# RWKV time mixing: input splits ahead of the keys, banks per first chunk, decays by group, the finish in pieces, and the gate's linears beside the last levels and the last state chain

## The chip, the cores and the metric

The kernel runs on one core of a Trainium2 chip. The metric is the device time of one execution in microseconds (us), as the median of several runs. Everything is computed in 32 bits; where this text says "split", a float32 operand is held as a rounded high part and the remainder (low part), and a product takes three matmuls (high x high, low x high, high x low).

## What is computed

One token sequence of 272 tokens (16 meta tokens and 256 inputs) and 1024 features goes through two blocks of feed-forward, mixer, feed-forward, and then through a third block with retention, convolution and sparse attention. The change touches only the first block's mixer, RWKV-7 time mixing:

```python
xx = pad(h)[:, :-1] - h
xr, xw, xk, xv, xa, xg = h + xx * mix[0..5]
r, k, v = xr @ w_r, xk @ w_k, xv @ w_v
w_log = -softplus(-(w0 + tanh(xw @ w1) @ w2)) - 0.5
a = sigmoid(a0 + (xa @ a1) @ a2)
g = sigmoid(xg @ g1) @ g2                       # the gate: two small linears
kk = normalized per head (k * k_k)
k = k * (1 + (a - 1) * k_a)
decay = exp(-exp(w_log))
y = wkv7_scan(r, decay, k, v, -kk, kk * a)      # 16 heads of 64, a 64x64 state each
yn = per-head layer norm of y, * lnx_g + lnx_b
bonus = sum(r * k * r_k) * v
out = ((yn + bonus) * g) @ w_o
```

## The kernel before

**Layout.** Features lie on the 128 partitions in 8 tiles, tokens (272) along the free axis. Weights come as one stream of 128x128 tiles, 16 to a slot, through a ring of four slots that the sync engine (SP) fills in order. For split linears ScalarE writes the high part of half a slot (8 weight tiles, `w_high`) and GpSimd (POOL) the low part (`w_low`); four such halves are buffered. One output tile of `rk_k`, `rk_r` or `rk_v` takes one half: 8 x 3 matmuls of 128x272. The small linears (`rk_w1`, `rk_w2`, `rk_a1`, `rk_a2`, `rk_g1`, `rk_g2`) use plain float32 matmuls out of the ring. Output tiles of these stages rotate through PSUM banks 0, 1, 2.

**Order.** Each engine runs a program written out by hand; semaphores join them. `PLAN` sets the order of the stages: w1, w2, a1, a2, k, r, v, g1, g2, o. `beside(host, guest)` interleaves two generators: the guest's piece behind `yield n` is issued once the host has made n steps.

**Inputs.** VectorE (DVE) makes the mixed inputs with `mix` (one SCALAR_TENSOR_TENSOR a tile), ScalarE (ACT) copies the high part (`mixed_high`), DVE subtracts for the low part (`mixed_low`). In the key stage DVE first makes the factor `1 + (a-1) k_a` for all tiles (L1889), then per key tile multiplies the product in PSUM (which frees the bank), mixes a tile of r, sums the decays' logarithms (L1899), and writes a low part of r. During r it does v's mixes and low parts, and the decays; then the gate's mixes. PE puts the heads' norms and the bonus (L853, L866, L877) between tiles of r and v.

**The scan.** Tokens are cut into chunks of 16, 128 and 128; heads into four groups g of four heads (two feature tiles). For a group and a chunk, `rk_turn` transposes inputs, `rk_score` makes the products, which DVE masks (`rk_mask`); all of these pass through banks 6 and 7. `rk_levels` inverts a triangular matrix by 7 levels of matmul, mask, matmul, add. Beside group g's levels run group g+1's turns and scores and group g-1's state chain: per chunk `rk_right`, `rk_solve`, `rk_update`, `rk_output`, which share bank 5, with copies by DVE and ACT between them. The last group's chain has no levels beside it. `rk_finish` (layer norm, bonus, gate) of group g is one run of DVE instructions; groups 0 and 1 have it beside the levels of groups 2 and 3, groups 2 and 3 behind the last chain. `rk_prepare` scales the inputs of all groups at once before the first turn.

## Time and profile before

| | us |
|---|---|
| median of 3 runs | 2350.32 (2349.2 to 2355.98) |
| the profiled execution's own time | 2356.69 |
| its span in the trace | 2354.9 |
| PE / DVE / ACT / POOL busy | 2160.2 / 874.2 / 917.7 / 1286.1 |

The profiled execution is 6.4 us above the median of the runs. Busy times are spans of instructions; matmuls overlap, so a PE that is busy is not always PE at its peak. Time mixing up to its output linear takes about 236 to 748 us of the span; behind it everything is as it was.

### The profile page before, as it was taken

Reading aid. Unit: us, or ns where it says so; the run is one execution under the profiler, and the core shown is the slowest. Engines: PE = TensorE matmul, PEld = TensorE weight load, DVE = VectorE, ACT = ScalarE, POOL = GpSimd, SP = SyncE. Lnnn points to the kernel's source line nnn. Section 1 sums busy time; section 2 is a strip of 40 time slices with the busy share of each in tenths; the row PEclk is TensorE's granted clock in tenths of the full one; section 3 lists DMA queues with packets and bytes.
Section 4 is the critical chain, followed back from the end, with each engine's and each line's share of the span. In section 5 each row is a group of like instructions: output and inputs, shape, how many; then the busy total and the mean of one; then the engine's idle time right before and its main releaser. Section 6 shows DMA issues by size and latency. Waiting matters only on the chain.

```text
span 2354.9 us, 41537 instructions
## 1 busy us (share of the span) xinstructions
PE 2160.2 (92%) x16520; PEld 2032.1 (86%) x16520; DVE 874.2 (37%) x1461; ACT 917.7 (39%) x1558; POOL 1286.1 (55%) x528
## 2 busy tenths in 40 slices
PE   5999778898887999999998789999999997999998
PEld 5999667788775899899988479999999887998997
DVE  3210764645643421132036526512144225323431
ACT  4433433001002434433344434444444554555552
POOL 4887242000003688588764029886774553576885
PEclk9999889999986999999999689999998998999999
DMA  5444221000001444345433025554445331344552
GB/s 222 176 171 160 94 103 72 1 2 1 1 1 72 143 178 174 130 179 178 173 132 108 1 72 179 184 191 162 143 162 197 126 126 72 124 146 145 191 184 89
DMA packets 40768, 292.11 MB, mean 124 GB/s; under 512 B 4416, under 2 KB 5568, under 8 KB 5568
## 3 DMA queue, kind: packets, MB, share of 16 engines
q1 hardware_dynamic: 40496, 289.18, 34.3%
q8 instruction: 101, 1.65, 0.3%
q10 hardware_dynamic: 144, 1.05, 0.1%
q14 instruction: 27, 0.22, 0.0%
HBM read 289.16 MB, written 1.05 MB: 123 GB/s over the span
## 4 chain that ended last, share of the span: by engine, by line
issue 34%; PE 29%; POOLq 17%; POOL 16%; ACT 1%; DVE 1%; DMA 1%; DVEq 0%; SPq 0%; ACTq 0%
POOLq L1719 17%; POOL w_low L1715 16%; PE ps L544 9%; PE ps L552 8%; PE ps L548 8%; PE ps L1142 2%; PE ps L1129 1%; PE ps L1119 1%; DMA wring<-stream 1%; PE ps L630 1%; POOLq L1714 0%; ACT units L1624 0%; ACT units L1207 0%; DVE rms L1757 0%; POOLq L1731 0%
## 5 line engine op out<-in xcount | busy, mean ns | idle before, releaser
L1715 POOL TENSOR_TENSOR w_low<-wring,w_high 128x1024 fp32r<-128x1024 f32 x524 | 1285.9, 2462 | 1047.6 <-ACT w_high L1207 1031.0
L544 PE MATMUL ps<-in_high,w_high 128*128 128x256 f32 (+1 forms) x2920 | 857.2, 294 | 44.5 <-DVE in_low L1741 38.1
L552 PE MATMUL ps<-in_high,w_low 128*128 128x256 f32 (+1 forms) x2920 | 843.4, 289 | 0.0
L548 PE MATMUL ps<-in_low,w_high 128*128 128x256 f32 (+1 forms) x2920 | 842.1, 288 | 0.0
L1207 ACT ACTIVATE w_high<-wring 128x1024 fp32r<-128x1024 f32 x524 | 548.9, 1056 | 442.7 <-PE ps L544 442.5
L544 PEld LDWEIGHTS ps<-in_high,w_high 128*128 128x128 f32 x2920 | 562.0, 192 | 58.2 <-issue 38.5
L548 PEld LDWEIGHTS ps<-in_low,w_high 128*128 128x128 f32 x2920 | 562.3, 193 | 0.6
L552 PEld LDWEIGHTS ps<-in_high,w_low 128*128 128x128 f32 x2920 | 562.9, 193 | 0.0
L544 PE MATMUL ps<-hid_high,w_high 128*128 128x272 f32 (+1 forms) x880 | 254.6, 289 | 0.0
L552 PE MATMUL ps<-hid_high,w_low 128*128 128x272 f32 (+1 forms) x880 | 250.4, 284 | 0.0
L548 PE MATMUL ps<-hid_low,w_high 128*128 128x272 f32 (+1 forms) x880 | 250.2, 284 | 0.0
L548 PEld LDWEIGHTS ps<-hid_low,w_high 128*128 128x128 f32 x880 | 165.7, 188 | 0.7
L544 PEld LDWEIGHTS ps<-hid_high,w_high 128*128 128x128 f32 x880 | 165.4, 188 | 0.7
L552 PEld LDWEIGHTS ps<-hid_high,w_low 128*128 128x128 f32 x880 | 165.5, 188 | 0.0
L1744 DVE SCALAR_TENSOR_TENSOR X<-ps,X 128x272 f32<-128x272 f32 (+1 forms) x64 | 27.7, 433 | 369.1 <-PE ps L552 369.1
L1741 DVE TENSOR_TENSOR hidden<-ps,silu_out 128x272 f32<-128x272 f32 (+1 forms) x88 | 38.5, 437 | 302.0 <-PE ps L552 302.0
L1207 ACT ACTIVATE AL<-ps 128x272 f32<-128x272 f32 (+5 forms) x91 | 37.8, 434 | 209.1 <-PE ps L773 75.4
L1741 DVE TENSOR_TENSOR hid_low<-hidden,hid_high 128x272 f32 (+1 forms) x88 | 107.8, 1225 | 12.9 <-issue 0.2
L1335 ACT ACTIVATE silu_out<-ps 128x272 f32<-128x272 f32 (+1 forms) x88 | 34.7, 395 | 156.7 <-PE ps L552 156.6
L1741 DVE TENSOR_TENSOR AL<-ps,AL 128x512 f32<-128x512 f32 (+4 forms) x69 | 47.3, 685 | 102.6 <-PE ps L702 59.1
L701 PE MATMUL ps<-AL,group 128*128 128x128 f32 (+1 forms) x384 | 70.8, 272 | 9.3 <-DVE AL L1741 9.3
L702 PE MATMUL ps<-group,AL 128*128 128x128 f32 (+1 forms) x480 | 77.6, 261 | 0.1
(267 smaller groups left out, 2676.1 us busy)
## 6 DMA issues: line engine op xcount, KB each, us to landing
wring<-stream SPq DMA_DIRECT2D x271, 1024.0 KB, 4.8
con<-consts SPq DMA_DIRECT2D x1, 2584.5 KB, 8.9
X<-x_in SPq DMA_DIRECT2D x1, 1088.0 KB, 11.5
units<-decay ACTq DMA_DIRECT2D x1, 1024.0 KB, 4.8
out<-AL SPq DMA_DIRECT2D x1, 1024.0 KB, 4.7
par<-params SPq DMA_DIRECT2D x1, 187.0 KB, 9.3
```

What stands on the lines that cost most here:

```text
L544: mm = pe.matmul(o, wh, high(k), start=(k == 0), stop=False)
L548: mm = pe.matmul(o, wh, low(k), start=False, stop=False)
L552: mm = pe.matmul(o, wl, high(k), start=False, stop=(k == kt - 1))
L701: pe.matmul(rk_level_bank(c, 1)[:, q, :], xt, y, start=True, stop=True)
L702: mm = pe.matmul(rk_level_bank(c, 2)[:, q, :], y, xt, start=True, stop=True)
L1142: mm = pe.matmul(ps[p:p + HD, 7, u * P:(u + 1) * P], v, pt[:, q, :], start=(i == 0), stop=(i == len(of_keys) - 1))
L1207: return act.activation(o, i, ACT.Copy, scale=scale)
L1335: act.activation(silu_out[:, p % 2, tokens], ps[:, (base + 2 * p) % 4, 0:size], ACT.Silu).then_inc(S["act_emptied"], 1)
L1715: pool.tensor_tensor(w_low[:, (half + h) % SPLIT_RING, :], wring[:, slot, h * HALF * P:(h + 1) * HALF * P], w_high[:, (half + h) % SPLIT_R ...
L1719: pool.drain()
L1741: return dve.tensor_tensor(o, a, b, op)
L1744: return dve.scalar_tensor_tensor(out=o, in0=a, scalar=scalar, in1=b, op0=op0, op1=op1)
```

## The change

Seven things move, all within time mixing:

- `rk_inputs` writes the mixes and both parts of k and r before the key stage's products: ACT copies six high parts of k ahead of `rk_a1`'s output, and the rest between `rk_a2`'s outputs. The gate's mixes stand ahead of the first key product on DVE. The factor is no longer made apart: a key tile takes two SCALAR_TENSOR_TENSORs with one operand in PSUM, and the bank is freed behind the second, which is issued after the next tile's first.
- v's mixes and the decays follow the keys; the norms' matmuls stand a tile later, the spread and the bonus a tile earlier.
- `rk_prepare(g)` works on one group: 0 and 1 before the first masks, 2 and 3 beside the first group's levels.
- The first group's three chunks have banks of their own (6, 0, 2), and their masks run in the order of products, then chunks. Buffers are laid out anew for it.
- `rk_finish` is three pieces (a reciprocal, a reciprocal, the rest) without the gate, beside the state chain of a later group; `rk_gate` multiplies by the gate straight from PSUM.
- `rk_g1` runs in eight pairs of matmuls beside the last group's levels, in banks 6 and 7; `rk_g2` runs a tile (two matmuls) at a time within the last state chain.
- In the last chain the state uses bank 7 and the output bank 6, and the output waits for `rk_sa` alone, not for the state.

The core of the diff:

```diff
-            def rk_prepare():
...
-                tt(B, B, T0[:, :, :], ALU.mult)
-                dve.wait_ge(S["rk_exps_ready"], 1)
-                stt(T0[:, :, :], T0[:, :, :], -1.0, T1[:, :, :], ALU.mult, ALU.mult)
...
+            def rk_prepare(g):
+
+
+                v = slice(2 * g, 2 * g + 2)
+                dve.drain()
+                tt(B[:, v, :], B[:, v, :], T0[:, v, :], ALU.mult)
+                tt(K[:, v, :], K[:, v, :], T2[:, v, :], ALU.mult)
+                yield
+                dve.drain()
+                stt(T0[:, v, :], T0[:, v, :], -1.0, T1[:, v, :], ALU.mult, ALU.mult)
+                tt(B[:, v, :], B[:, v, :], T2[:, v, :], ALU.mult)
+                yield
+                tt(R[:, v, :], R[:, v, :], W[:, v, :], ALU.mult).then_inc(S["rk_prepared"], 1)
+                yield
...
+                for k in range(DT):
+                    mix("g", G[:, k, :], k)
+
+
+                dve.wait_ge(*emptied("rk_a2", 7))
                 for k in range(DT + 1):
+                    tile = tiles_before[stage_number("rk_k")] + k
+                    u = ps[:, BANK[tile], 0:T]
+                    dve.drain()
                     if k < DT:
...
+                        dve.wait_ge(S["rk_kk_squared"], k + 1)
+                        stt(K[:, k, :], B[:, k, :], -1.0, u, ALU.add, ALU.mult)
+                        dve.tensor_tensor_scan(W[:, k, :], const("reset"), W[:, k, :], 0.0, ALU.mult, ALU.add)
                     if k:
...
+                        u = ps[:, BANK[tile - 1], 0:T]
+                        stt(K[:, k - 1, :], K[:, k - 1, :], param("k_a")[:, k - 1:k], u, ALU.mult, ALU.add
+                            ).then_inc(S["dve_emptied"], 1)
...
             def rk_finish(g):
 
-                Y = A[:, 8 + 2 * g:10 + 2 * g, :]
+
                 dve.wait_ge(S["rk_y_rooted"], g + 1)
-                dve.reciprocal(rk_inv, rk_root)
+                for u in range(2):
+                    dve.reciprocal(rk_root[:, u, :], rk_root[:, u, :])
+                    yield
...
+            def rk_gate(*tiles):
...
+                    tt(A[:, 8 + k, :], ps[:, BANK[tile], 0:T], A[:, 8 + k, :], ALU.mult).then_inc(S["dve_emptied"], 1)
...
-            linear("rk_g1", lambda k: A[:, 40 + k, :], before_k=lambda k: pe.wait_ge(S["rk_mixed_g"], k + 1))
-            pe.wait_ge(*emptied("rk_g1", 1))
-            linear("rk_g2", lambda k: rk_lora[:, k, :])
-            pe.wait_ge(*emptied("rk_g2", 7))
-            pe.wait_ge(S["rk_prepared"], 1)
+            pe.wait_ge(*emptied("rk_v", 7))
+            pe.wait_ge(S["rk_bonus_read"], 2)
             for c in range(3):
                 rk_turn(0, c)
-                for i in range(2):
+            for i in range(2):
+                for c in range(3):
                     rk_score(0, c, i)
             for g in range(4):
                 beside(rk_levels(g), rk_beside(g))
+            pe.wait_ge(*emptied("rk_g1", 1))
+            for c in (1, 2):
+                pe.wait_ge(S[f"rk_x{c}_added"], 4 * RK_COUNT[c])
+            gate = linear_by_two("rk_g2", lambda k: rk_lora[:, k, :])
             for c in range(3):
                 rk_right(3, c)
+                next(gate)
                 rk_solve(3, c)
+                next(gate)
                 if c < 2:
                     rk_update(3, c)
                 rk_output(3, c)
             rk_mean(3)
+            next(gate)
             rk_variance(3)
...
+            def linear_by_two(name, rhs):
...
+                for i in range(nt):
+                    tile = tiles_before[s] + i
+                    bank_free(tile)
+                    for k in range(kt):
+                        w = weight_tile(PLAN_STARTS[s] + i * kt + k)
+                        mm = pe.matmul(ps[:, BANK[tile], 0:T], w, rhs(k), start=(k == 0), stop=(k == kt - 1))
...
+                        if k % 2:
+                            yield
...
+                gate = linear_by_two("rk_g1", lambda k: A[:, 40 + k, :]) if g == 3 else iter(())
                 for c in range(3):
                     if g:
                         yield 7 * c
                         rk_right(before, c)
-                    if c and g < 3:
+                    if c:
                         yield 7 * c + 1
-                        rk_turn(after, c - 1)
+                        next(gate, None)
+                        if g < 3:
+                            rk_turn(after, c - 1)
...
+            def rk_banks(g, c):
+
+
+                return 6 if g else (6, 0, 2)[c]
...
-                if c < 2:
+                if c < 2 and g < 3:
                     pe.wait_ge(S["rk_state_ready"], g * 2 + c + 1)
                 else:
                     pe.wait_ge(S["rk_sa_copied"], 3 * g + c + 1)
+                if c and g == 3:
+                    pe.wait_ge(S["rk_y_copied"], 3 * g + c)
...
```

**DVE in the key stage.** These are its rows before, from the factor on (`AL` holds all the block's tiles, `par` the parameters, `con` constants such as `reset`; the L1899 rows are the sums of the decays' logarithms):

```order
L1889 TENSOR_SCALAR AL<-AL,par,small 128x272 [waits act_emptied]
L1889 TENSOR_SCALAR AL<-AL,par,small 128x272 x7
L1741 TENSOR_TENSOR AL<-ps,AL 128x272 [waits rk_kk_squared]
L1744 SCALAR_TENSOR_TENSOR AL<-AL,par 128x272
L1899 SCALAR_TENSOR_TENSOR AL<-con,AL 128x272
L1741 TENSOR_TENSOR AL<-ps,AL 128x272 [waits rk_kk_squared]
L1744 SCALAR_TENSOR_TENSOR AL<-AL,par 128x272
L1899 SCALAR_TENSOR_TENSOR AL<-con,AL 128x272
L1741 TENSOR_TENSOR r_low<-AL,r_high 128x272 [waits rk_high]
```

And of the change, from the gate's mixes on (the L1993 rows are those sums now):

```order
L1820 SCALAR_TENSOR_TENSOR AL<-AL,par 128x272 x8
L1820 SCALAR_TENSOR_TENSOR AL<-AL,ps 128x272 [waits act_emptied,rk_kk_squared]
L1993 SCALAR_TENSOR_TENSOR AL<-con,AL 128x272
L1820 SCALAR_TENSOR_TENSOR AL<-AL,ps 128x272 [waits rk_kk_squared]
L1993 SCALAR_TENSOR_TENSOR AL<-con,AL 128x272
L1820 SCALAR_TENSOR_TENSOR AL<-AL,par,ps 128x272
L1820 SCALAR_TENSOR_TENSOR AL<-AL,ps 128x272 [waits rk_kk_squared]
L1993 SCALAR_TENSOR_TENSOR AL<-con,AL 128x272
L1820 SCALAR_TENSOR_TENSOR AL<-AL,par,ps 128x272
```

The factor and r's mix and low part are gone from the tile's round; the gate's eight mixes stand ahead of it, and the instruction that frees a bank follows the next tile's first one.

**DVE at the finish.** Before, the finish of group 1 within the last levels, between two masks of a level:

```order
L1741 TENSOR_TENSOR AL<-ps,con 128x512 [waits rk_under1_ready]
L2028 RECIPROCAL AL<-AL 128x544 [waits rk_y_rooted]
L1741 TENSOR_TENSOR AL<-AL 128x544
L2033 TENSOR_SCALAR AL<-AL,par 128x272 x2
L1741 TENSOR_TENSOR AL<-AL 128x544 x2
L1741 TENSOR_TENSOR AL<-ps,con 128x512 [waits rk_under2_ready]
```

Of the change, the last state chain, with the finish of group 2 (the RECIPROCALs) and the gate's products (`ps,AL` 128x272) between the chain's copies and states:

```order
L2087 COPY in_parts<-ps 16x256 [waits rk_z_ready]
L2112 RECIPROCAL in_parts<-in_parts 128x272 [waits rk_y_rooted]
L1817 TENSOR_TENSOR small<-ps,small 128x256 [waits rk_s_ready]
L1817 TENSOR_TENSOR AL<-ps,AL 128x272 [waits linear_ready] x2
L2087 COPY in_parts<-ps 128x256 [waits rk_z_ready]
L2112 RECIPROCAL in_parts<-in_parts 128x272
L1817 TENSOR_TENSOR small<-ps,small 128x256 [waits rk_s_ready]
L1817 TENSOR_TENSOR small<-small 128x256
L1817 TENSOR_TENSOR AL<-ps,AL 128x272 [waits linear_ready] x2
L2087 COPY in_parts<-ps 128x256 [waits rk_z_ready]
```

The whole reciprocal no longer stands ahead of a mask; a half of it stands behind each copy that PE's `rk_solve` waits for.

**PE in the last state chain, chunk 1.** Before, from the end of `rk_right` over `rk_solve` (L742) and `rk_update` (L754, L755) to the first row of `rk_output`:

```order
L731 MATMUL ps<-small,AL 128x64
L742 MATMUL ps<-group 128x64 [waits rk_x1_added,rk_z_copied]
L742 MATMUL ps<-group 128x64 x3
L754 MATMUL ps<-group 64x64 [waits rk_sa_copied]
L755 MATMUL ps<-group 64x64
L754 MATMUL ps<-group 64x64
L755 MATMUL ps<-group 64x64
L754 MATMUL ps<-group 64x64
L755 MATMUL ps<-group 64x64
L754 MATMUL ps<-group 64x64
L755 MATMUL ps<-group 64x64
L770 MATMUL ps<-group 64x128 [waits rk_state_ready]
```

Of the change, the same place (L593 is `rk_g2`):

```order
L789 MATMUL ps<-in_parts 128x64 x3
L593 MATMUL ps<-rms,wring 128x272 [waits dve_emptied]
L593 MATMUL ps<-rms,wring 128x272
L801 MATMUL ps<-in_parts,AL 64x64 [waits rk_sa_copied]
L802 MATMUL ps<-AL 64x64
L801 MATMUL ps<-in_parts,AL 64x64
L802 MATMUL ps<-AL 64x64
L801 MATMUL ps<-in_parts,AL 64x64
L802 MATMUL ps<-AL 64x64
L801 MATMUL ps<-in_parts,AL 64x64
L802 MATMUL ps<-AL 64x64
L819 MATMUL ps<-AL,in_parts 64x128 [waits rk_sa_copied,rk_y_copied]
```

Two matmuls of the gate's second linear now stand between solve and update (two more between right and solve), and the output waits for the copy of `sa`, not for the state.

## Rows read from the trace of the kernel before

**Rows 1.** Windows by stage: length, busy time (instructions) per engine, PEclk, DMA share, GB/s.

```profile
core 0: us, PE busy (x) PEld busy (x) DVE busy (x) ACT busy (x) POOL busy (x), PEclk, DMA share, GB/s
265.86:384.84 118.98, 99.12 (x627) 88.62 (x628) 86.89 (x100) 50.93 (x88) 60.95 (x22) 0.89 0.32 115
384.84:400.40 15.56, 14.50 (x63) 11.39 (x62) 4.40 (x8) 5.26 (x11) 0.00 (x0) 1.00 0.18 67
400.40:421.76 21.36, 13.55 (x73) 8.91 (x73) 5.46 (x6) 2.59 (x6) 0.00 (x0) 0.62 0.00 1
421.76:471.76 50.00, 45.09 (x429) 40.90 (x428) 33.55 (x60) 2.60 (x6) 0.00 (x0) 0.99 0.01 1
544.57:620.10 75.53, 66.46 (x597) 59.18 (x595) 43.03 (x75) 6.08 (x14) 0.00 (x0) 0.93 0.01 1
620.10:689.85 69.75, 60.05 (x531) 54.17 (x529) 38.03 (x69) 3.48 (x8) 0.00 (x0) 0.90 0.00 1
```

**Rows 2.** Timeline of PE: start, length, instruction, idle before and its releaser.

```profile
280.36 0.39 PE L544 MATMUL ps<-in_high,w_high 128*128 128x272 f32 x1 [2.73 <-DVE AL L1741]
302.36 0.39 PE L544 MATMUL ps<-r_high,w_high 128*128 128x272 f32 x1 [3.89 <-DVE r_low L1741]
331.19 3.96 PE L866 MATMUL ps<-rms,group 16*128 16x272 f32 x8 [3.34 <-DVE rms L1922]
```

**Rows 3.** Timeline of ACT: two outputs of r, one PE tile apart.

```profile
315.78 0.40 ACT L1207 ACTIVATE AL<-ps 128x272 f32<-128x272 f32 x1 [1.78 <-PE ps L552]
318.80 0.40 ACT L1207 ACTIVATE AL<-ps 128x272 f32<-128x272 f32 x1 [1.36 <-PE ps L552]
```

**Rows 4.** Timeline of DVE and POOL in the key stage.

```profile
280.22 0.49 DVE L1744 SCALAR_TENSOR_TENSOR AL<-AL,par 128x272 f32<-128x272 f32 x1
280.63 0.71 DVE L1899 TENSOR_TENSOR_SCAN AL<-con,AL 128x272 f32<-128x272 f32 x1
...
282.64 2.58 DVE L1741 TENSOR_TENSOR r_low<-AL,r_high 128x272 fp32r<-128x272 f32 x1
...
292.70 0.43 DVE L1741 TENSOR_TENSOR AL<-ps,AL 128x272 f32<-128x272 f32 x1
...
282.21 2.71 POOL L1715 TENSOR_TENSOR w_low<-wring,w_high 128x1024 fp32r<-128x1024 f32 x1 [3.24 <-ACT w_high L1207]
...
292.36 2.66 POOL L1715 TENSOR_TENSOR w_low<-wring,w_high 128x1024 fp32r<-128x1024 f32 x1 [0.50 <-issue]
```

**Rows 5.** Timeline of DVE: a mask of the first group.

```profile
407.68 1.23 DVE L1741 TENSOR_TENSOR in_parts<-ps,con 128x1024 f32<-128x1024 f32 x1 [4.04 <-PE ps L673]
```

**Rows 6.** Timelines of DVE and PE: finish of group 0, and PE behind two finishes.

```profile
595.08 3.54 DVE L2028 RECIPROCAL AL<-AL 128x544 f32<-128x544 f32 x1
598.70 0.72 DVE L1741 TENSOR_TENSOR AL<-AL 128x544 f32<-128x544 f32 x1
...
602.60 0.46 PE L701 MATMUL ps<-AL,group 128*128 128x128 f32 x2 [3.76 <-DVE AL L1741]
...
674.06 0.77 PE L701 MATMUL ps<-AL,group 128*128 128x128 f32 x2 [5.27 <-DVE AL L1741]
```

**Rows 7.** Windows of the last chain: chunk 0, 1, 2, and the tail.

```profile
689.85:695.02 5.17, 3.08 (x40) 2.74 (x41) 0.82 (x3) 0.57 (x2) 0.00 (x0) 0.73 0.00 0
695.02:711.49 16.47, 13.87 (x64) 10.65 (x64) 1.28 (x3) 0.75 (x3) 0.00 (x0) 0.50 0.00 1
711.49:725.44 13.95, 12.29 (x48) 9.26 (x48) 1.12 (x3) 1.41 (x6) 0.00 (x0) 0.50 0.00 0
725.44:747.89 22.45, 7.45 (x26) 5.75 (x26) 16.98 (x19) 5.49 (x12) 4.65 (x2) 0.58 0.24 94
```

**Rows 8.** Timeline of PE and DVE: the head means twice (L782), the centring, the output linear's start.

```profile
679.87 1.08 PE L782 MATMUL ps<-AL,con 128*128 128x272 f32 x4
...
725.50 2.18 PE L782 MATMUL ps<-AL,con 128*128 128x272 f32 x4 [0.47 <-ACT AL L1207]
...
734.67 0.72 DVE L1744 SCALAR_TENSOR_TENSOR AL<-ps,AL 128x544 f32<-128x544 f32 x1
...
747.89 0.59 PE L544 MATMUL ps<-in_high,w_high 128*128 128x272 f32 x1 [6.49 <-DVE in_low L1741]
```

312 lines of the change are left out of this document (172 added, 140 removed).

## The prediction

> **What bounds the kernel now.** I read the page's totals first, which only say that PE is the busiest engine, and then the windows, cut at the stages of time mixing, because a reordering is worth what its own stage waits for. [rows 1] gives the lengths: 119 us for keys, receptance and values, 15.6 for the gate's two linears, 21.4 for the first group's turns, products and masks, then levels 0 (50.0), 2 (75.5) and 3 (69.8); levels 1 are left as they are. [rows 7] gives the last chain in three chunks and a tail, 58.0 us in all. What the reader is to see is how far PE's work is from each length.
>
> In the first stage an output tile takes PE 3.02 us when nothing stops it, the distance of the two outputs in [rows 3]. 24 tiles are 72.5 us. The 24 matmuls of norms and bonus are plain float32; 32 such matmuls fill the gate's window of 15.56 us [rows 1], waits included, so I take 0.46 each, 11.0 us. That is 83.5 us of work in 119. The difference is waiting for DVE, as the timeline's releasers say: for a bank, for r's low parts, for the inverse norm [rows 2]. Why is DVE late? [rows 4]: an instruction of 0.4 us, r's low part, took 2.58 us while POOL ran a `w_low` of 2.71. But the key product, one operand in PSUM, took 0.43 beside another of 2.66. So POOL and DVE instructions with two operands in SBUF exclude each other here.
>
> In the mask stage PE is at half clock (0.62 mean) and waits for masks that share two banks: a mask takes 1.23 us and DVE had been idle 4.04 before it [rows 1, 5]. In levels 2 and 3 PE is nearly always busy, except behind the finish: 3.76 and 5.27 us [rows 6], the second followed by matmuls at half clock (0.77 against 0.46 us). The last chain runs at 0.50 [rows 7]: the same four records of head means take 2.18 us there and 1.08 in the levels [rows 8].
>
> **The change, part by part.** *Keys to the first turn, now 134.5 us (265.86 to 400.40).* The start stays near 265.5, since ACT's outputs of `rk_a2` share their time with the high parts and pace PE. Then no split is waited for. But DVE has eight gate mixes ahead of the first key product, each with two SBUF operands (0.49 us, [rows 4]), from about 269 on, just when four halves of `w_low` (2.4 us each) follow each other. One or two fit between two halves, so they end near 280. The first bank is free behind product, sum, product, sum, product: 0.43 + 0.71 + 0.43 + 0.71 + 0.43, and drains and one blocked sum: 284. PE wants it for the fourth tile at 265.5 + 3 x 3.02 = 274.5. A stall of 9.5 us, and 2 us for a fall of the clock behind it. After that the per-tile round on DVE is 1.6 us and a wait for POOL, under 3.02 most of the time. In r, the inverse norm now needs v's mixes, the decays and six low parts first; that chain I put at 2.5 us behind PE. Behind the last value tile: its copy, a bonus product of 1.3 us, 2 us with the hops. Sum 83.5 + 11.5 + 2.5 + 2 = 99.5, with the 0.4 us of the earlier start 99.9: **-34.6 us**. In it lie the 15.6 us of the gate, which are put back below. Bounds: without the first stall 88; with each of the 22 halves costing PE 0.5 us, 110.
>
> *Masks, now 21.4 us.* DVE needs 4.6 us first (the second group's scaling, 5 instructions of 0.65, and small ones; 0.65 is the 0.72 of [rows 6] less overlap), in which PE, without masks to wait for, turns and scores. Then four masks of 1.23, two of 0.28, and one wait: 10.3 us. **-11.1 us**.
>
> *Levels 0.* Groups 2 and 3 are scaled there: 10 instructions of 0.65 on DVE, 6.5 us, in the first two levels where DVE itself is last. I laid them between the masks by their order; the second level's masks come 4.4 us later. **+4.4**, between 2 and 6.5.
>
> *Levels 2.* The finish's one block (3.54 for the reciprocal, 0.72 and more behind it [rows 6]) becomes halves of 1.8 us, placed where DVE waits for PE. Of PE's 3.76 us and some 1.7 of half clock I give back 1: **-4.5**. *Levels 3* likewise, 5.3 + 1.8 less 0.8, **-6.3**, and the first gate linear is put in: PE has no gap near it, so 16 x 0.46 = **+7.3**.
>
> *Last chain.* The second gate linear puts 6 tiles of two matmuls (0.92 us at full clock, 1.9 to 2.2 at half [rows 8]) between PE's steps, where PE now waits 0.5 to 1 us for DVE or ACT. Output and its copy leave the loop: PE does the output while DVE makes the state. In the tail, the centring no longer stands behind group 2's finish: today the means end at 727.7 and the centring starts at 734.67 [rows 8]; and the gate's product is 2 x 0.43 at its end.
> At full clock: chunk 0 about 5.0 with two gate tiles; chunk 1 (13.87 busy at half, so 6.9, less waits) with two tiles about 9.3; chunk 2 about 8.4; tail 11.5 (means 1.1, centring 0.8, variance 2, root 0.8, finish 5.1, gate and split 1.7): 34. At half clock: 6.6, 17.9, 16.2, tail 14: 55. Which? In [rows 7] chunk 1 is busy 13.87 of 16.47 us at 0.50 and the clock doesn't come back; these matmuls are only 64 columns long or fill half the array. The gate's tiles are full ones, 272 columns. I take the drop in chunk 0, as now, and the return with chunk 1's gate tiles: 5.0 + 17.9 + 8.4 + 0.5 + 11.5 = 43.3. **-14.7**, between -3 and -24.
>
> A rule on this, which the sum doesn't need: the Trainium skill, "TensorE: Matmul & The Clock Gate", section "HAM oscillation — how this bites in real kernels", says that waits between bursts put the clock back to its lower rate again and again. By that rule the chain, which keeps its waits, is at half throughout: the half-clock rival below. The trace before agrees with it, at 0.50 for the chain.
>
> Sum: -34.6 - 11.1 + 4.4 - 4.5 - 6.3 + 7.3 - 14.7 = **-59.5 us**. Against the profiled execution, 2356.7, this is 2297; against the median of the runs, 2350.3, it is **2291**, which I give. Weights cost nothing: the output linear's last slot was and is loaded when that linear starts, and six output tiles, 18 us of PE work, come before its use.
>
> **Rivals.**
> *The last chain stays at half clock.* It takes 55 and not 43.3: 2303. For it: 0.50 in [rows 7] despite 84% busy. Against: there were no full matmuls there.
> *The port.* DVE's chain through v's mixes, the decays and the low parts meets a `w_low` at each step. The keys lose 8 us more (eight sums of 0.71 each behind a half of 2.4 give a round of 4.0, not 3.0) and the inverse norm 3: 2302. For it: [rows 4]. A rule bears on it: the Trainium skill, "SBUF — State Buffer", section "Who interferes with whom", says that of a DVE instruction with two SBUF inputs and a GpSimd one, whichever issues first holds the port throughout. The trace agrees, 2.58 us for a low part; by the rule alone the round is 4.0 whenever POOL issues first. Both rivals together: 2314.
> *Better.* The clock holds in the chain (-9), and the mixes slip through before the halves (-10): 2272.
> *Slower than before.* Short stalls for banks, spread over the first stage, keep PE at its lower clock for the whole of it: 83.5 us of work become 167, with 12 us of stalls 179, in place of 99.9. That is +79 on 2291, 2370. It decides from the point where the stage takes 159 us, over nine tenths of it at half clock. Against: [rows 1] has 0.89 in this stage today with longer stalls.
> *No change*: each wait removed is replaced by another of its length. It would take three stages doing so at once.
>
> **How the numbers follow.** 2291 as summed 0.48; half clock in the chain 0.20; port 0.13; both 0.05; better 0.11; slower 0.02; no change 0.01. The range takes in all of these but the far side of the better case, the far side of both rivals together, and the slower one: **2271 to 2312**. A difference under 0.3% (7 us) can't be told from none in this kernel. Faster 0.97, same 0.01, slower 0.02.
>
> **What would show it.** First stage: one long wait of PE for a bank in the keys, near the fourth tile, some 10 us; no wait for `r_low`; first turn near 365. Masks in 10 us, levels starting near 376. Levels 0 near 54 us; no wait over 2 us for DVE in levels 2 and 3; levels 3 about as long as before, with 32 records of `rk_g1`. The last chain in 40 to 46 us with the clock column back to 1 in its second half. Wrong would be: waits of PE for DVE of 2 us in many key tiles (the port), a chain over 52 us at 0.5 (the clock), or a wait in the chain for a gate product on DVE.

## The result, and the profile after

The changed kernel takes 2293.9 us (median of 4 runs, 2288.9 to 2294.5) against 2350.0 before: a ratio of 0.974, 95% interval 0.972 to 0.9765. The prediction was 2291. The profiled execution took 2294.1 us with a span of 2292.2, 62.7 less than the span of before. Its windows, cut at the same instructions as [rows 1] and [rows 7]: keys, receptance and values up to the first turn (called the first stage below), masks, levels 0, 1, 2, 3; then chunks 0, 1, 2 of the last chain, and its tail.

```profile
268.73:374.85 106.12, 92.35 (x626) 86.08 (x626) 67.05 (x84) 48.16 (x81) 54.69 (x22) 0.90 0.37 129
374.85:387.56 12.71, 10.22 (x80) 8.13 (x81) 10.57 (x19) 2.33 (x6) 0.00 (x0) 0.87 0.01 1
387.56:441.72 54.16, 45.98 (x422) 41.79 (x420) 38.72 (x70) 2.59 (x6) 0.00 (x0) 0.94 0.00 1
441.72:512.20 70.48, 64.45 (x597) 57.22 (x595) 36.83 (x68) 7.35 (x15) 0.00 (x0) 0.95 0.00 1
512.20:587.77 75.57, 69.54 (x597) 62.14 (x595) 41.95 (x74) 6.07 (x14) 0.00 (x0) 0.89 0.00 1
587.77:657.14 69.37, 64.84 (x564) 57.88 (x562) 37.23 (x68) 6.83 (x12) 0.00 (x0) 0.95 0.00 1
...
657.14:661.28 4.14, 4.13 (x48) 3.06 (x48) 2.60 (x3) 0.37 (x1) 0.00 (x0) 1.00 0.55 190
661.28:670.44 9.16, 9.16 (x73) 7.20 (x74) 4.61 (x8) 1.96 (x5) 2.36 (x1) 1.00 0.08 30
670.44:678.91 8.47, 8.43 (x56) 6.40 (x56) 5.84 (x10) 2.35 (x6) 2.36 (x1) 1.00 0.01 3
678.91:690.13 11.22, 4.20 (x17) 2.88 (x17) 7.66 (x12) 2.73 (x7) 0.00 (x0) 0.88 0.00 0
```

Against the prediction's terms (us; levels 1 take 72.8 before, the distance of two borders of [rows 1]; the last chain is counted from DVE's copy of its first right side, at 657.14):

| stage | before | after | measured | predicted |
|---|---|---|---|---|
| keys to first turn | 134.5 | 106.1 | -28.4, start 1.7 later: -26.7 | -34.6 |
| masks | 21.4 | 12.7 | -8.7 | -11.1 |
| levels 0 | 50.0 | 54.2 | +4.2 | +4.4 |
| levels 1 | 72.8 | 70.5 | -2.3 | 0 |
| levels 2 | 75.5 | 75.6 | 0.0 | -4.5 |
| levels 3 | 69.8 | 69.4 | -0.4 | -6.3 + 7.3 |
| last chain | 58.0 | 33.0 | -25.0 | -14.7 |
| sum | | | -58.9 | -59.5 |

A residual is DVE's addition of a finished output tile to the block's running sum. Time mixing from its first to its last residual is 57.3 us shorter (541.4 to 484.1, the end taken at the output linear's last residual, 774.97 and 718.77 us); the other 5.4 of the 62.7 lie in code that is the same in both.

That the sum is right is luck: its two largest errors cancel. The first stage gives 7.9 us less than forecast, the last chain 10.3 more. The other stages together give 3.0 less. The start is the first key matmul's distance to the last residual before time mixing, 34.06 us here and 32.33 before. It isn't the change's: among the kernels below, whose code is the same up to there, it is one or the other.

The waits of PE in the first stage, and of the same view in the levels up to 657 us, by line, with sum, number and longest:

```profile
PE ps L562 <- DVE AL L1820: 8.0, 1, 8.0
PE ps L927 <- DVE rms L2014: 3.0, 1, 3.0
...
PE ps L789 <- DVE in_parts L2087: 10.6, 3, 3.5
```

The first is the wait for a bank at the fourth key tile, the second the one for the inverse norm, which was 3.34 us in [rows 2]. The wait for r's low part is gone. So is the longest wait of this stage before, which neither the prediction nor its rows show. Timelines of DVE and PE in the kernel before:

```profile
345.74 3.39 DVE L1744 SCALAR_TENSOR_TENSOR AL<-AL,par 128x272 f32<-128x272 f32 x8
349.05 1.28 DVE L1741 TENSOR_TENSOR AL<-ps,AL 128x1088 f32<-128x1088 f32 x1
350.47 3.06 PE L866 MATMUL ps<-rms,group 16*128 16x272 f32 x6 [6.60 <-DVE AL L1741]
```

PE waited 6.60 us there for DVE's scaling at 349.05, and about 3.3 of them went to the same eight gate mixes, which then stood ahead of that scaling. The change took them away from one thing that PE waits for and put them ahead of another, the bank of the fourth key tile.

The third line shows three waits of 3.52 us in levels 1, 2 and 3, for the copy of the first right side. They were there before the change, and the prediction didn't look at them. The two waits behind the finish [rows 6] are gone.

Timeline of DVE and POOL at the first two key tiles:

```profile
272.07 11.84 DVE L1820 SCALAR_TENSOR_TENSOR AL<-AL,par 128x272 f32<-128x272 f32 x8
284.01 0.44 DVE L1820 SCALAR_TENSOR_TENSOR AL<-AL,ps 128x272 f32<-128x272 f32 x1
...
272.59 5.20 POOL L1791 TENSOR_TENSOR w_low<-wring,w_high 128x1024 fp32r<-128x1024 f32 x2 [40.26 <-ACT w_high L1275]
278.05 5.15 POOL L1791 TENSOR_TENSOR w_low<-wring,w_high 128x1024 fp32r<-128x1024 f32 x2 [0.26 <-issue]
```

Eight gate mixes of 0.49 us take 11.84 beside four halves of `w_low`, and the first key product starts at 284.01. The prediction had the mixes end near 280 and the first bank free at 284; the bank came free, and PE resumed, at 286.68.

### The profile page after: what moved, and what is told of

It reads as the page before. It is cut to its first block, busy times and chain, and to the rows that moved or that the text cites. A ratio compares the mean times of both kernels' runs of the same rounds, so it can differ in the third digit from the quotient of the medians.

```text
span 2292.2 us, 41543 instructions
## 1 busy us (share of the span) xinstructions
PE 2130.0 (93%) x16520; PEld 2010.9 (88%) x16520; DVE 866.4 (38%) x1483; ACT 915.1 (40%) x1551; POOL 1279.5 (56%) x528
## 4 chain that ended last, share of the span: by engine, by line
issue 32%; PE 29%; POOLq 18%; POOL 17%; ACT 1%; DVE 1%; DMA 1%; DVEq 0%; SPq 0%; ACTq 0%
POOLq L1795 17%; POOL w_low L1791 17%; PE ps L562 9%; PE ps L570 9%; PE ps L566 9%; PE ps L1210 2%; PE ps L1197 1%; PE ps L1187 1%; DMA wring<-stream 1%; PE ps L670 1%; POOLq L1790 0%; ACT units L1700 0%; ACT units L1275 0%; DVE rms L1833 0%; POOLq L1807 0%
## 5 line engine op out<-in xcount | busy, mean ns | idle before, releaser
L562 PE MATMUL ps<-in_high,w_high 128*128 128x256 f32 (+1 forms) x2856 | 834.5, 292 | 41.0 <-DVE in_low L1817 30.1
L570 PE MATMUL ps<-in_high,w_low 128*128 128x256 f32 (+1 forms) x2856 | 823.1, 288 | 0.0
L566 PE MATMUL ps<-in_low,w_high 128*128 128x256 f32 (+1 forms) x2856 | 821.7, 288 | 0.0
L562 PEld LDWEIGHTS ps<-in_high,w_high 128*128 128x128 f32 x2856 | 547.8, 192 | 51.5 <-issue 38.4
L570 PEld LDWEIGHTS ps<-in_high,w_low 128*128 128x128 f32 x2856 | 548.8, 192 | 0.0
L566 PEld LDWEIGHTS ps<-in_low,w_high 128*128 128x128 f32 x2856 | 548.5, 192 | 0.3
L1817 DVE TENSOR_TENSOR group<-ps,group 128x512 f32<-128x512 f32 (+1 forms) x78 | 44.8, 600 | 62.2 <-PE ps L744 62.1
L670 PE MATMUL ps<-normed,con 128*128 128x272 f32 (+1 forms) x144 | 44.1, 415 | 20.1 <-ACT normed L1294 19.5
L1351 ACT ACTIVATE units<-ps 128x256 f32<-128x256 f32 x69 | 26.4, 383 | 85.3 <-PE ps L570 85.2
## 6 DMA issues: line engine op xcount, KB each, us to landing
X<-x_in SPq DMA_DIRECT2D x1, 1088.0 KB, 11.5
```

The lines of the kernel that those rows point to most:

```text
L562: mm = pe.matmul(o, wh, high(k), start=(k == 0), stop=False)
L566: mm = pe.matmul(o, wh, low(k), start=False, stop=False)
L570: mm = pe.matmul(o, wl, high(k), start=False, stop=(k == kt - 1))
L670: mm = pe.matmul(ps[:, 4, 0:size], ones, normed[:, k, T - size:T], start=(k == 0), stop=(k == DT - 1))
L1351: act.activation(put(i), ps[:, BANK[tile], 0:size], func(i)).then_inc(S["act_emptied"], 1)
L1817: return dve.tensor_tensor(o, a, b, op)
```

## The experiments

Each edit is made on the changed kernel. The ratio is to the kernel before, run beside it on the same chip; the changed kernel's own is 0.974. Stage lengths are taken from the profiles by the same borders. They show a moved wait more sharply than the ratio does, for a reason that belongs here: from the output linear's last residual to the end all these kernels are the same, and in their profiles this stretch takes 1561 to 1580 us. Two whole times therefore differ by some us without a cause in the edit. Stage lengths of a single profile vary too. Where the code up to the masks is the changed kernel's, the first stage took 106 us in four profiles, 105.2, 102.4 and 99.4 in one each; the last chain, unaltered, took 33.0 in three and 34.65 in five. The waits mostly repeat from profile to profile, but the time for which the clock falls behind them doesn't. So the waits and the clock are read below, and a stage length only beside them.

**The keys: gate mixes, one per key tile.**

```diff
-                for k in range(DT):
-                    mix("g", G[:, k, :], k)
...
                         stt(K[:, k - 1, :], K[:, k - 1, :], param("k_a")[:, k - 1:k], u, ALU.mult, ALU.add
                             ).then_inc(S["dve_emptied"], 1)
+                        mix("g", G[:, k - 1, :], k - 1)
```

> The changed kernel with the eight gate mixes taken from ahead of the first key product and put one into each key tile's round on DVE, behind the tile's second product. Theory (POOL holds DVE): the mixes took 11.84 us as a block only because each found a half of w_low running; without them the first product comes at the first key tile (273.4 us), PE has no wait for a bank at the fourth key tile (8.04 us now), and the clock stays at full there (10.24 us at half now, which cost some 3 us). The round becomes 0.44 + 0.72 + 0.47 + 0.43 = 2.1 us, at worst 4.4 where a half of w_low holds it, against PE's 3.03. Time 8 to 11 us under the changed kernel, 2283 to 2286. Rival (the held instructions only move): a mix in each round waits for the half of w_low that runs there, the round comes near 4 us, and what is saved at the fourth tile is lost in the others: 2290 to 2296.

Measured 2290.9 us, ratio 0.972 (0.970 to 0.974). The first stage takes 103.3 us for 106.1, which is no more than this stage varies without an edit. By the waits, the rival held. Timeline of DVE, one key tile's round:

```profile
277.78 0.44 DVE L1820 SCALAR_TENSOR_TENSOR AL<-AL,ps 128x272 f32<-128x272 f32 x1
278.13 2.35 DVE L1989 TENSOR_TENSOR_SCAN AL<-con,AL 128x272 f32<-128x272 f32 x1
280.41 0.47 DVE L1820 SCALAR_TENSOR_TENSOR AL<-AL,par,ps 128x272 f32<-128x272 f32 x1
280.80 2.17 DVE L1820 SCALAR_TENSOR_TENSOR AL<-AL,par 128x272 f32<-128x272 f32 x1
```

The two products, with an operand in PSUM, take 0.44 and 0.47. The running sum (0.72 alone) and the mix (0.49 alone), with both in SBUF, each wait for a half of `w_low`. The round is 5.3 us where PE needs 3.03, and PE waits four times, 5.2 us in all. The Trainium skill, "SBUF — State Buffer", section "Who interferes with whom", says that of such a DVE instruction and one of GpSimd's, the later waits in full; the trace agrees for these two, and for the products, which it lets pass.

**The inverse norm earlier.**

```diff
-                    if k == 5:
+                    if k == 2:
                         dve.wait_ge(S["rk_kk_rooted"], 1)
```

> The changed kernel with the reciprocal of the key norms on DVE behind three of v's low parts, and no longer behind six. Now the root is ready at 320.70 us and the reciprocal starts at 324.33, because the four low parts ahead of it took 7.61 us beside POOL's w_low; PE waits 2.96 us for it and has its clock at half for 10.24 us from there. Theory: the reciprocal starts right behind the root, near 320.8, the wait is gone and the clock stays at full; 3 us of wait and 3 of half clock, 2287 to 2290. Rival: the clock falls there whatever the wait, because the spread's matmuls have 16 rows only; the wait alone goes, 2291 to 2292. Second rival: v's low parts come later and PE waits for them at v's first tile instead; no change, 2293 to 2295.

Measured 2288.7 us, ratio 0.970 (0.968 to 0.973). The first stage takes 98.6 us, 7.5 less, and has one wait over 2 us left. So in that profile the 2.96 us wait had cost 7.5: behind it the clock was at half for 10.24 us, and is at full here. The first theory held. It isn't a fixed price: behind the same wait of 2.96 us, the clock was at half for 10.2 us in five profiles, 6.8 in three and 3.4 in one. The window of the fallen clock, in the changed kernel:

```profile
325.50:335.74 10.24, 9.43 (x32) 8.03 (x33) 3.05 (x4) 1.06 (x1) 3.47 (x2) 0.51 0.27 102
```

**The gate mixes behind v's**, on top of that, with the decays behind v's low parts:

```diff
                     mix("v", mixed[:, k, :], k)
+                for k in range(DT):
+                    mix("g", G[:, k, :], k)
...
+                for k in range(DT):
+                    mixed_low(2, k, mixed, in_high, in_low)
+                    if k == 2:
...
                 for c, (t0, C) in enumerate(CHUNKS):
                     ins = tt(W[:, :, t0:t0 + C], W[:, :, t0:t0 + C], tiles_of(rk_mid[:, c, :], DT, C), ALU.subtract)
```

> The kernel with the inverse behind three low parts, and further the eight gate mixes moved out of the keys altogether, to behind v's mixes, where POOL has no w_low to split; the clamp and v's low parts then come ahead of the decays. In the kernel with one gate mix per key tile the round of DVE was 5.2 us while POOL's halves followed each other: the running sum took 2.35 us and the mix 2.17. Theory (two held instructions per round are one too many, and one is affordable): with the mixes gone from the keys, a round is 0.44 + 2.35 + 0.47 = 3.3 us at the most, the 8.04 us stall is gone, and keys to first turn goes from 98.6 (inverse moved alone) to 86 to 90 us; time 9 to 12 us under that kernel's, a ratio to the kernel before of 0.965 to 0.967. Rival (the port limits the keys anyway): the sums held by every half of w_low keep the round over 3.03 us and short waits stay, 2 to 5 us gained, 0.968 to 0.970. Second rival: the mixes behind v's delay the inverse, and PE's wait of 3 us comes back.

Measured 2282.0 us, ratio 0.968 (0.966 to 0.970). The first stage takes 97.9 us, only 0.7 less than the one before it. The 8.04 us wait is down to 1.51, yet 3.20 us came up at the second half of the spread, and the clock fell there:

```profile
313.15 6.13 DVE L1817 TENSOR_TENSOR in_low<-in_parts,in_high 128x272 fp32r<-128x272 f32 x5
319.38 4.75 DVE L1817 TENSOR_TENSOR AL<-AL,small 128x128 f32<-128x128 f32 x3
324.05 1.28 DVE L1817 TENSOR_TENSOR AL<-ps,AL 128x1088 f32<-128x1088 f32 x1
```

The scaling at 324.05, for which PE waits, stands behind eight instructions with two SBUF operands. So part of the stall had not been removed but moved. A third kernel put the decays, 4.78 us of them, ahead of the reciprocal instead, only two and three of v's low parts ahead of the two scalings, and the last three behind everything.

**The same, with the decays ahead of the reciprocal and the low parts spread:**

```diff
+                dve.wait_ge(S["rk_kk_rooted"], 1)
+                dve.reciprocal(rms[0:16, 0, :], rms[0:16, 1, :]).then_inc(S["rk_kk_inv"], 1)
                 for half in range(2):
+                    for k in ((0, 1), (2, 3, 4))[half]:
+                        mixed_low(2, k, mixed, in_high, in_low)
...
+                for k in (5, 6, 7):
+                    mixed_low(2, k, mixed, in_high, in_low)
```

> The kernel with the gate mixes behind v's mixes once more, but with the decays directly behind the mixes and the clamp, the reciprocal right behind them, and v's low parts spread between and behind the two scalings of the spread norms. In the kernel with the mixes behind v's, the first stall had gone (8.04 to 1.51 us), yet 3.20 us came back at the second half of the spread, because the decays took 4.75 us between two halves of w_low and stood, with five held low parts (6.13 us), ahead of the scaling; and the clock fell there, not in the keys. Theory: with nothing of the two sorts ahead of the reciprocal and the scaling, PE has no wait over 1.6 us up to the first turn, the clock stays at full, and keys to first turn takes 88 to 92 us (97.9 in that kernel, 106.1 in the changed one), ratio 0.964 to 0.967. Rival (whatever is taken from one place waits at another, as the number of held instructions is the same): 96 to 98 us, ratio 0.968 to 0.970.

Measured 2274.3 us, ratio 0.967 (0.965 to 0.970). The first stage, in its window:

```profile
265.75:356.60 90.85, 85.96 (x625) 80.32 (x625) 67.85 (x84) 48.26 (x81) 57.52 (x22) 1.00 0.43 151
```

90.9 us at a clock of 1.00, in the range of the theory, 15.3 under the changed kernel's. No wait up to the first turn is longer than 1.51 us. The kernel with all moves, further below, has the same 90.85 us. As many instructions with two SBUF operands as before are in the stage, so what they cost depends on who waits behind them. Part of the lower median (19.6 us) is again outside the edit: levels 2, unaltered, took 70.9 us.

**The gate linears back before the first turn**, out of levels 3 and of the chain:

```diff
+            linear("rk_g1", lambda k: A[:, 40 + k, :], before_k=lambda k: pe.wait_ge(S["rk_mixed_g"], k + 1))
+            pe.wait_ge(*emptied("rk_g1", 1))
+            linear("rk_g2", lambda k: rk_lora[:, k, :])
...
-            gate = linear_by_two("rk_g2", lambda k: rk_lora[:, k, :])
...
-                    tt(A[:, 8 + k, :], ps[:, BANK[tile], 0:T], A[:, 8 + k, :], ALU.mult).then_inc(S["dve_emptied"], 1)
+                    tt(A[:, 8 + k, :], A[:, 40 + k, :], A[:, 8 + k, :], ALU.mult).then_inc(S["rk_gated"], 1)
```

> The changed kernel with only the gate's part undone: both gate linears stand between values and the first turn, as before, their results are copied to SBUF by ACT, and levels 3 and the last state chain have no gate tiles. Theory (full gate tiles keep the clock): the gate's stage comes back with 15.6 us, levels 3 get 6 to 7 us shorter, and the chain, 33.0 us now with 9.5 us of gate tiles in it at a granted clock of 1.00, falls to half clock as in the kernel before and takes 40 to 45 us without them: sum +15.6 - 7 + 7 to 12, 2309 to 2315. Rival (the new order and the second bank keep the clock, by taking the waits for the state out): the chain stays at 1.00 and takes 24 to 27 us: 2295 to 2298.

Measured 2317.4 us (2298.4 to 2317.8), ratio 0.981 (0.976 to 0.986), above the 2309 to 2315 of the theory. Windows of levels 3 and of the chain up to the output linear's first matmul:

```profile
601.31:664.50 63.19, 57.98 (x531) 52.14 (x529) 36.95 (x69) 3.48 (x8) 0.00 (x0) 0.95 0.00 1
664.50:701.52 37.02, 31.77 (x160) 24.22 (x161) 13.15 (x25) 6.57 (x15) 4.69 (x2) 0.53 0.00 1
```

Without the gate tiles the chain is at half clock (0.53), as it was before the change, and the output linear then waits 4.48 us more, to 709.96: 45.5 us, in place of 33.0 with 9.1 us of gate tiles in them. Counted to the last residual of the output linear it is 72.1 against 61.6. The first stage is 14.1 us longer, levels 3 are 6.2 shorter. By this profile the theory held: without the gate's tiles the clock is down, with them it is up. And it isn't down for waits alone: from 674.78 to 686.00 PE has no wait at all, with matmuls of 64 and 128 columns, and the clock is at 0.50 throughout. Two things stay open. One of the four runs took 2298.4 us at a mean granted clock of 0.951, the others 2317.0 to 2317.8 at 0.939 and 0.940; it has no profile, so what its chain did isn't known. And no kernel filled the gaps with small matmuls, so a full matmul and a mere filling of the gap are not told apart.

**The chain with one bank and the old order**, gate tiles kept:

```diff
-                return (7, 6) if g == 3 else (5, 5)
+                return (5, 5)
...
-                if (g or c) and (g < 3 or c == 0):
+                if g or c:
...
-                if c < 2 and g < 3:
+                if c < 2:
```

> The changed kernel with the last state chain's banks and order put back: solve, update and output share one bank, the output waits for the state, and the next right side waits for the output's copy; the gate tiles stay in the chain. Theory (the gate tiles keep the clock, the order is a small matter): the clock stays at 1.00, each of chunks 0 and 1 gets the state's hop (1.0 us) and the copy's (0.6 us) back, the chain takes 35.5 to 37 us in place of 33.0: 2 to 4 us slower than the changed kernel, ratio 0.975 to 0.976. Rival (both are needed): with the longer waits the clock falls in the chain, which takes 42 to 48 us, ratio 0.978 to 0.981.

Measured 2295.3 us, ratio 0.974 (0.973 to 0.976). Windows of chunks 0, 1, 2 and the tail:

```profile
647.32:652.80 5.48, 4.50 (x49) 3.34 (x49) 3.38 (x5) 0.72 (x3) 0.00 (x0) 1.00 0.50 191
652.80:667.23 14.43, 12.76 (x72) 10.07 (x73) 3.82 (x6) 2.03 (x5) 2.35 (x1) 0.76 0.01 1
667.23:675.78 8.55, 8.51 (x56) 6.48 (x56) 5.22 (x10) 1.82 (x4) 2.35 (x1) 1.00 0.01 3
675.78:687.00 11.22, 4.20 (x16) 2.87 (x16) 7.66 (x12) 2.73 (x7) 0.00 (x0) 0.88 0.00 0
```

39.7 us, between the two expectations. The clock falls at 653.66, in chunk 1, and comes back at 660.49, before the chunk ends; it then stays up through a wait of 1.11 us at 662.87, longer than any wait in the profile above, without gate tiles, up to the variance (0.6 us). So the banks and the order are worth up to 6.7 us. Part of these are not theirs: in three of the kernels above, with the changed kernel's chain, the clock also fell at its start, for 3.4 us, and the chain took 34.65. The ratio can't tell this kernel from the changed one, since the first stage (102.4) and levels 2 (72.5) came out shorter in it without an edit there.

**The output linear's first tile in a bank of its own:**

```diff
+                elif name == "rk_o":
+                    BANK.append(3 - i % 4)
```

> The changed kernel with the output linear's tiles in banks 3, 2, 1, 0 and not 0, 1, 2, 3 in their count over the plan, so that its first tile has a bank that no gate tile holds. Now its first matmul waits 5.99 us for DVE's last gate products. Theory: PE does the first 18 of 24 matmuls of that tile (six input tiles are split by then), 2.3 us at full clock, in the wait; what is left of the wait is under 4 us and the clock's fall from 687 to 694 us comes later or not at all: 2 to 6 us gained, ratio 0.972 to 0.973. Rival: the matmuls before the last two input tiles only move, the clock falls in the rest of the wait, and the first tile's end, which waits for the last low parts, is less than 1.5 us earlier: 0.9735 to 0.975.

Measured 2283.5 us (2279.3 to 2295.3), ratio 0.970 (0.967 to 0.974). PE does 18 matmuls from 683.70 to 686.3 and waits 4.66 us for the last low parts; the first residual is 2.5 us earlier, the last 1.7 (from the first key matmul on). Neither expectation is met as a whole. The clock falls later and for 3.4 us, not 6.8, as in the theory; but the wait left is over its 4 us, and the tiles that follow wait for `w_low`, so that the last residual gains less than its 2 us. The rest of the lower median lies behind time mixing, in the 1561 us of this profile, and isn't the edit's as far as the trace tells.

**The copy of the first right side behind one chunk:**

```diff
-                        yield 7 * c + 1
+                        yield 7 * c + (1 if c else 0)
                         rk_right(before, c)
```

> The changed kernel with DVE's copy of the first chunk's right side, in levels 1 to 3, behind one chunk of the first level instead of two. PE waits 3.52, 3.52 and 3.52 us for that copy in the three groups (10.6 us in all), and in levels 2 it is at half clock for 17 us from there. Theory (this wait is where the gain expected of levels 2 went): each wait shrinks by the 2.6 us of one chunk's four instructions, 7.8 us, and the fall in levels 2 is gone, 4 to 8 us more: 2279 to 2287. Rival: PE comes to wait for the second chunk's first level instead, which stands 0.4 us later, and nothing is gained: 2292 to 2296.

Measured 2280.4 us, ratio 0.967 (0.964 to 0.970). Levels 1, 2 and 3:

```profile
440.71:508.08 67.37, 63.91 (x597) 56.78 (x595) 36.74 (x69) 7.36 (x15) 0.00 (x0) 0.97 0.01 1
508.08:575.69 67.61, 62.62 (x597) 55.35 (x595) 41.61 (x74) 6.07 (x14) 0.00 (x0) 1.00 0.01 1
575.69:643.50 67.81, 65.66 (x564) 58.54 (x563) 36.92 (x69) 6.84 (x12) 0.00 (x0) 0.95 0.00 1
```

3.1, 8.0 and 1.6 us less; the three waits are 0.95 us each. In levels 2 the granted clock is now 1.00 throughout. That is where the gain expected of levels 2 had gone: at the wait of 3.52 us the clock fell and was at half for 17 us. Before the change, at the same wait, it was at half for 6.8.

**The finish in one block again:**

```diff
-                    if g >= 2:
-                        yield 7 * c + 2
-                        next(finish)
...
+                if g >= 2:
+                    yield 21
+                    for _ in finish:
+                        pass
```

> The changed kernel with the finish of groups 0 and 1 in one block again, at the place where it stood (behind the chunks' copies, ahead of the last masks). In the changed kernel levels 2 take 75.6 us, no less than before, and levels 3 69.4 with 16 gate matmuls in them. Theory (the pieces took the wait away, but another fall of the clock, behind the 3.52 us wait for the first right side, ate the gain in levels 2): with the block back, waits of 3.8 and 5.3 us come back, levels 2 take 78 to 80 us and levels 3 75 to 77: 8 to 11 us slower, ratio 0.978 to 0.979. Rival (the finish was hidden anyway, PE's wait behind it only seemed to cost): 0 to 3 us slower, 0.974 to 0.9755.

Measured 2304.7 us, ratio 0.978 (0.977 to 0.980). Levels 2 take 78.8 and levels 3 74.4 us, with waits of 2.53 and 3.32 us behind the block and a fall of the clock behind each. That is 3.2 and 5.1 us over the changed kernel, near the theory, though the waits are shorter than its 3.8 and 5.3 and levels 3 are 0.6 under its range. The chain is 4.6 us longer too, since a fall of the clock lies in it.

**The scaling of groups 2 and 3 ahead of the masks:**

```diff
-                for _ in rk_prepare(1):
-                    pass
+                for g in (1, 2, 3):
+                    for _ in rk_prepare(g):
+                        pass
```

> The changed kernel with the scaling of groups 2 and 3 (10 instructions on DVE) put back ahead of the first masks, out of levels 0. Theory (the scaling costs in levels 0 what was summed for it, +4.4 us, as DVE is last in the first two levels, and it would cost its full 6.5 us ahead of the masks, where PE waits for DVE): masks take 12.7 + 6.5 = 19 us, levels 0 go from 54.2 to 50 us, 2 us slower in all, ratio 0.975 to 0.976. Rival (levels 0 grew for another reason, the half clock of 7 to 10 us near 394 to 401 us): levels 0 stay at 53 to 54 us, the whole is 6 us slower, 0.977 to 0.978.

Measured 2292.6 us, ratio 0.974 (0.972 to 0.976). Masks 19.65 and levels 0 49.99 us, both as in the theory: 2.8 us more for the two. The whole didn't get slower, because of something that this edit doesn't touch. The first stage took 99.4 us, as DVE's eight gate mixes were not held: they took 3.39 us, and POOL's `w_low` waited for them. PE waited 2.76 us for `w_low` in its place, and not 8 for the fourth bank. Timeline of DVE and POOL there:

```profile
270.80 3.39 DVE L1820 SCALAR_TENSOR_TENSOR AL<-AL,par 128x272 f32<-128x272 f32 x8
...
271.33 7.81 POOL L1791 TENSOR_TENSOR w_low<-wring,w_high 128x1024 fp32r<-128x1024 f32 x2 [39.98 <-ACT w_high L1275]
```

**The changed kernel once more**, to see whether these things vary by themselves.

> The changed kernel once more, unaltered, with a profile of its own. In one experiment whose code up to the masks is the changed kernel's, DVE's eight gate mixes took 3.39 us and POOL's first half of w_low waited for them (5.3 us in place of 2.4), where in six others they took 11.8 us behind POOL; and levels 2 took 75.6 us in three profiles and 72.5 in three others, with the same instructions. Theory (both differ from one execution to the next, and no edit causes them): one of the two again comes out other than in the first profile, and where the first stage has the mixes at 3.39 us it takes 99 us and not 106; the median stays at a ratio of 0.972 to 0.976. Rival (the edit decides, the first profile repeats): mixes of 11.8 us, first stage 106 us, levels 2 75.6 us, to 0.1 us.

Measured 2294.3 us, ratio 0.976 (0.974 to 0.9775). Windows of the first stage and of levels 2:

```profile
268.22:374.21 105.99, 92.23 (x625) 85.96 (x625) 67.08 (x84) 48.18 (x81) 54.78 (x22) 0.90 0.36 130
511.55:587.10 75.55, 69.52 (x597) 62.11 (x595) 41.95 (x74) 6.06 (x14) 0.00 (x0) 0.89 0.00 1
```

106.0 and 75.6, mixes of 11.84 us: it repeats to 0.1 us. The rival held. The theory that they vary from one execution to the next has nothing for it from these two profiles. That leaves it unexplained why the kernel with the scaling ahead (99.4 us), and the one with one bank in the chain (102.4), differ in the first stage, with the same instructions up to the masks. In the latter DVE, POOL and the waits are as in the changed kernel, and only the falls of the clock behind the two waits are shorter, 6.8 and 3.4 us for 10.2 and 10.2.

**All moves together**: keys as in the kernel of 90.9 us, the copy behind one chunk, the bank of its own.

> The three moves that gained, together: gate mixes, decays, reciprocal and low parts in the order of the kernel without mixes in the keys; the copy of the first right side behind one chunk in levels 1 to 3; the output linear's first tile in a bank of its own. If they add up: 14 to 18 us in the first stage, 11 in the levels and 3 at the output linear, 28 to 32 us under the changed kernel, ratio to the kernel before 0.960 to 0.963. If they share the same falls of the clock and so overlap: 18 to 24 us, 0.964 to 0.967.

Measured 2267.9 us (2265.7 to 2269.5, 5 runs), ratio 0.963 (0.961 to 0.965), the fastest of all. By the profile the moves nearly add up: from the first key matmul to the last residual of the output linear it takes 421.0 us, the changed kernel 450.0, so 29.0 less, where the three alone give 16.8 (15.3 of it in the first stage) + 10.8 + 1.7 = 29.3. The ratio, at 0.963 against 0.974, gives some 26 us.

## Why the prediction was right, and where not

*First stage, -34.6, measured -26.7.* The sum has a slip: a start at 265.5 and 99.5 us give a first turn at 365.0, 35.4 before 400.40, since an earlier start adds to the gain. The start at 265.5 was one of two values that occur (1.7 us). The stall at the fourth tile was predicted at 9.5 us plus 2 for the clock, and was 8.04, but both of its ends were off: the mixes began at 272.07 and not near 269, so that the bank came free at 286.68 for 284, and PE asked for it at 278.64 for 274.5. The mechanism was right, the nearness of the size is partly luck. The term that was mis-sized is the inverse norm, "2.5 us behind PE": the wait is 2.96, but it costs 7.5 in this profile, because the clock falls behind it. The step that failed priced a wait by its own length. With that wait gone the stage is at 98.6, 0.9 from the 99.5 that were summed from the first key matmul on. The reading of the stage before, waits for a bank, for r's low parts and for the inverse norm, left out the longest, 6.60 us for the scaling behind the gate's mixes. Of the 28.4 us between the two profiles 15.6 are the gate's own stage, which is moved and not saved; 6.1 are idle time of PE, and 6.8 less busy time.

*The port rival.* It was right as a mechanism and wrong in its place. In the changed kernel only one instruction per key round is held, the round is affordable, and no tile waits after the fourth. With a second held instruction the rival came true (four waits, 5.2 us). Of another rival, *slower than before*, the deciding point is reckoned wrong: with its 12 us of stalls, 83.5 us of work make a stage of 159 us when four fifths of it, not nine tenths, are at half clock.

*Masks, -11.1, measured -8.7*, and *levels 0, +4.4, measured +4.2*. Taking the scaling out of levels 0 makes them 50.0 us again and the masks 19.7. Of the 4.2 us, 3.3 are more idle time of PE and 0.9 more busy time, with the clock at half for 6.8 us in these levels. The 2.4 us missing in the masks were not tested; in the window PE has two waits for masks, 0.9 and 1.3 us, where one was expected, and the clock is at 0.87.

*Levels 1, forecast as unchanged, measured -2.3.* Nothing was changed there, and PE's waits are the same. The clock is at half for 6.8 us in the changed kernel's profile and for 10.2 in the one before, which is 1.7 of the 2.3.

*Levels 2 and 3.* The prediction read PE as nearly always busy there except behind the finish; a wait of 3.52 us stood in each, before and after. The finish's block costs 3.2 and 5.1 us as measured by putting it back, for 4.5 and 6.3. The first came to nothing in the profile, since a fall of the clock of 17 us in levels 2 stood against it (in five kernels with the same code there it was 10.2 us, and levels 2 took 72.5 to 72.7); the one before the change had 0.93 there, this one 0.89. Levels 3 with the first gate linear are 6.2 us longer than without, for 7.3.

*The last chain, -14.7, measured -25.0*, outside the term's own bounds of -3 and -24. The working at full clock, 5.0, 9.3, 8.4 and 11.5, met three of the four windows, 9.2, 8.5 and 11.2, within 0.3 us; chunk 0 took 4.1. 1.7 us of the gain are chance, as the same chain took 34.65 in five other profiles. What failed was the choice "I take the drop in chunk 0, as now, and the return with chunk 1's gate tiles". The clock didn't drop before the tail. The rule weighed there, from the Trainium skill, "TensorE: Matmul & The Clock Gate", section "HAM oscillation — how this bites in real kernels", of waits that put the clock back, foretold half clock in the chain. The section's own case is longer waits, for DMA; in the chain before the change none was over 1.11 us up to the variance, so it bore on this case only loosely. It has nothing to act on here: the gate's tiles fill the waits, and PE has one left of 0.5 us from 657.14 to 682. But short waits are not all that holds the clock down: without gate tiles PE's longest wait up to the variance is 0.6 us, the clock is at 0.53, and it stays at half through 11.2 us without any wait. What differs there is the work: these matmuls are 64 or 128 columns long, many of them on half the array, the gate's are 272 long and fill all of it. Whether that or the mere filling of the gaps made the difference was not tested apart. One gain was read too well: the chain ends at the output linear's resumption, and before the change that tile had three quarters of its matmuls done by then; now it had none, since its bank was held by a gate tile, and 1.6 us go by the second tile.

## What to carry to other kernels

Price a wait of PE with the fall of the clock behind it: here 3 us of waiting cost up to 7.5, so a short wait is worth more than its length, and by how much varies between kernels. Look for independent full matmuls to fill a chain's gaps: here the chain's own work then ran at the full clock, and the filler was more than paid for. Where two engines exclude each other, order the queue so that nothing that can be held stands ahead of what the bounding engine waits for; taking a stall away at one place without that only moves it.

## What was unexpected of the hardware

*Filling 9.1 us of full matmuls into a chain made it 12.5 us shorter* (33.0 against 45.5, or 10.5 counted to the output linear's last residual), at clocks of 1.00 in the three chunks and 0.53 up to the output linear.

*The length of a fall of the clock is not fixed.* At the same 3.52 us wait in levels 2, the granted clock was at half for 17.1 us in the changed kernel, both times, and for 10.2 in the kernel with the inverse earlier, with the same instructions in these levels: 75.6 and 72.6 us. Before the change it was 6.8. What decides was not found.

*Who holds the SBUF is not settled by a single instruction.* POOL's first `w_low` began 0.5 us behind DVE's first mix in all nine profiles with the block of eight mixes. In eight of them the first two mixes took 0.49 us each, POOL's half got in behind them and took 2.65, and the two engines then took turns, four of the other six mixes taking some 2.6 us; the block took 11.8 us. In one, that with the scaling ahead, the block took 3.39, and two halves of `w_low` took 7.81 in place of 5.20, so that POOL waited through the whole block. Why this one profile differs stays open.
